# A two-layer hybrid trunk on one core: the triangular inversion starts from 8x8 blocks solved on VectorE, and taps and a rounding go to ScalarE

## The reference

```python
h = rmsnorm(x); proj = h @ w_in          # q,k,v | g_out | a,b | glu | gates
q,k,v = silu(causal_depthwise_conv(qkv, 4 taps)); q,k = l2norm
o = gated_delta_chunked(q, k, v, g, beta)      # 8 heads of width 128
y_a = (rmsnorm(o) * silu(g_out)) @ w_a_out
c = val * sigmoid(gt); c = causal_depthwise_conv(c, 31 taps) + bias
y_b = silu(rmsnorm(c)) @ w_b_out
x = x + (sigmoid(gate_a) * y_a + sigmoid(gate_b) * y_b) @ w_o

# inside gated_delta_chunked, per head and chunk:
m = (k*beta) @ k.T * decay_strict              # strictly lower triangular
sol = triangular_solve(eye + m, [v*beta | k*beta*exp(gc)])
```

## Time and profile before

| | us |
|---|---|
| median of 3 runs | 2707.73 (2707.4 to 2707.75) |
| span of the profiled execution | 2705.9 |
| TensorE busy | 2695.0 |
| VectorE busy | 1583.0 |
| ScalarE busy | 1099.9 |
| GpSimd busy | 257.8 |

### The profile page before, as it was taken

How to read it: one execution, slowest core, us unless ns; L and a number is a source line. 1 busy time by engine, 2 the same in 40 slices (tenths; PEclk the granted TensorE clock), 3 DMA queues, 4 the chain that set the end, 5 groups by cost and what they waited for, 6 DMA issues and landing times.

```text
span 2705.9 us, 35838 instructions
## 1 busy us (share of the span) xinstructions
PE 2695.0 (100%) x13096; PEld 2251.8 (83%) x13096; DVE 1583.0 (59%) x2505; ACT 1099.9 (41%) x1849; POOL 257.8 (10%) x231
## 2 busy tenths in 40 slices
PE   9999999999999999999999999999999999999998
PEld 7888878888888888888888888788888888888887
DVE  6554357888885345554355543688888944455532
ACT  4222246766663232222222222566666633322222
POOL 0000022122120010000000000221211200100000
PEclk9999999999999999999999999999999999999999
DMA  4223335564552223233322233455556432232331
GB/s 167 95 99 104 92 102 141 126 142 115 136 130 93 100 86 101 93 101 94 103 93 93 101 93 95 109 133 137 125 128 141 102 109 96 90 101 93 97 95 66
DMA packets 83482, 292.04 MB, mean 108 GB/s; under 512 B 10032, under 2 KB 10800, under 8 KB 83376
## 3 DMA queue, kind: packets, MB, share of 16 engines
q1 hardware_dynamic: 68112, 235.85, 27.0%
q0 software_dynamic: 14976, 54.53, 11.0%
q10 hardware_dynamic: 288, 0.27, 0.0%
HBM read 233.99 MB, written 2.10 MB: 87 GB/s over the span
## 4 chain that ended last, share of the span: by engine, by line
PE 99%; issue 0%; DVE 0%; DMA 0%; DVEq 0%; SPq 0%; POOLq 0%; ACT 0%; POOL 0%
PE bank L451 97%; PE bank L650 1%; PE bank L702 1%; PE bank L664 0%; PE bank L738 0%; DMA xT<-in_x 0%; PE bank L471 0%; DVE NT L1683 0%; DVE XT L1688 0%; DVE h_lo L1276 0%; DVE y L1351 0%; PE bank L814 0%; DVEq L120 0%; POOLq L120 0%; ACT h_hi L891 0%
## 5 line engine op out<-in xcount | busy, mean ns | idle before, releaser
L1251 DVE TENSOR_TENSOR w_lo<-raw,w_hi 128x1024 fp32r<-128x1024 f32 x342 | 422.8, 1237 | 535.4 <-ACT w_hi L868 535.4
L868 ACT ACTIVATE w_hi<-raw 128x1024 fp32r<-128x1024 f32 x446 | 470.0, 1055 | 651.1 <-PE bank L451 651.0
L451 PE MATMUL bank<-h_hi,w_hi 128*128 128x512 f32 x1504 | 587.5, 391 | 1.1 <-issue 0.6
L451 PE MATMUL bank<-h_hi,w_lo 128*128 128x512 f32 x1504 | 585.6, 389 | 0.0
L451 PE MATMUL bank<-h_lo,w_hi 128*128 128x512 f32 x1504 | 585.3, 389 | 0.0
L451 PE MATMUL bank<-g_hi,w_hi 128*128 128x512 f32 x928 | 382.1, 412 | 0.0
L451 PE MATMUL bank<-g_hi,w_lo 128*128 128x512 f32 x928 | 377.8, 407 | 0.0
L451 PE MATMUL bank<-g_lo,w_hi 128*128 128x512 f32 x928 | 369.4, 398 | 0.0
L451 PEld LDWEIGHTS bank<-h_hi,w_hi 128*128 128x128 f32 x1504 | 282.4, 188 | 63.0 <-issue 2.3
L451 PEld LDWEIGHTS bank<-h_hi,w_lo 128*128 128x128 f32 x1504 | 282.3, 188 | 58.9
L1554 DVE SCALAR_TENSOR_TENSOR cacc<-c_raw,ncol,cacc 128x512 f32<-128x512 f32 x464 | 330.3, 745 | 0.4
(11 more groups left out here) (256 smaller groups left out, 3352.4 us busy)
## 6 DMA issues: line engine op xcount, KB each, us to landing
raw<-in_w_in SPq DMA_DIRECT2D x128, 512.0 KB, 3.3
w_lo<-raw POOLq DMA_DIRECT2D x104, 512.0 KB, 4.6
raw<-in_ffn_w_up SPq DMA_DIRECT2D x88, 512.0 KB, 3.3
raw<-in_ffn_w_gate SPq DMA_DIRECT2D x87, 512.0 KB, 3.3
raw<-in_ffn_w_down SPq DMA_DIRECT2D x64, 512.0 KB, 3.5
raw<-in_ffn_w_down SPq DMA_DIRECT2D x32, 384.0 KB, 3.1
raw<-in_w_a_out SPq DMA_DIRECT2D x16, 512.0 KB, 3.3
raw<-in_w_b_out SPq DMA_DIRECT2D x16, 512.0 KB, 3.3
```

The costliest lines, as they stand in the source:

```text
L451: return nc.tensor.matmul(o, a, b, start=start, stop=stop, **kw)
L868: nc.scalar.activation(w_hi[c % SLOTS][:, :], raw[c % SLOTS][:, :], ACT.Copy).then_inc(hi_done, 1)
L1251: tt(w_lo[c % SLOTS][:, :], raw[c % SLOTS][:, :], w_hi[c % SLOTS][:, :].bitcast(F32), ALU.subtract).then_inc(lo_v, 1)
```

## The change

Levels 0 and 1 go. `BASE` = 2: level 2 finds in bank 0 the inverses of the 8x8 diagonal blocks, made thus: ScalarE copies the 32x32 diagonal blocks of NT (*near*, four copies of 32 partitions each), VectorE masks them to the 8x8 blocks (*diag*), sums them into rows (*cin*) and spreads them over a unit pattern (*own*, 256 elements); one TensorE product with the block mask (*rows*) gives every partition its block's rows in bank 2; back substitution by VectorE (z7, then z6p, z6a to z1p, z1a on 4 to 28 elements) gives X, and X0 writes it to bank 0. Late taps are put between these steps (`inside`, `ahead`), `LATE` becomes 10. The taps 0 and 1 of the long convolution (`first_taps`) and o's rounding (`o_round`) are done by ScalarE, after XT of level 3. attnT and "c" move behind level 2. The constants lose two masks and get one. `transpose`s of `gr` become matmuls with the same operands and one accumulation group.

```diff
-PE_ORDER = "H H gr kt H kk kq H so H H H x2t vt H H H xt0 y0 H H fb xy0".split()
-for _l in range(1, LEVELS):
-    PE_ORDER += ("H H H " if _l < LEVELS - 1 else "H H H H ").split() + f"xt{_l} y{_l} H H H xy{_l}".split()
+PE_ORDER = "H H gr kt H kk kq H so H H H rows vt H H H H H H fb H H H H H H H H".split()
+for _l in range(BASE, LEVELS):
+    PE_ORDER += ("H H H " if BASE < _l < LEVELS - 1 else "H H H H " if _l == LEVELS - 1 else "").split() + f"xt{_l} y{_l} H H H xy{_l}".split()
 PE_ORDER += "H H H xtf H H H vn0 H H os0".split()
 for _c in range(1, NC):
     PE_ORDER += f"H H p{_c} H H vn{_c} H H H os{_c}".split()
 HALVES = 12
-LATE = 8
+LATE = 10
...
-DVE_STEPS = ["hs", "kT", "qT", "dmin", "skE", "rden", "bnk2", "neg", "NT", "x2T", "vT", "yd0", "attnT"]
-DVE_STEPS += [f"yd{_l}" for _l in range(1, LEVELS)]
+DVE_STEPS = ["hs", "kT", "qT", "dmin", "skE", "rden", "bnk2", "neg", "NT", "vT", "diag", "cin", "own"]
+DVE_STEPS += [f"z{SIDE - 1}"] + [f"z{_k}{_x}" for _k in range(SIDE - 2, 0, -1) for _x in "pa"] + ["X0", f"yd{BASE}", "attnT"]
+DVE_STEPS += [f"yd{_l}" for _l in range(BASE + 1, LEVELS)]
 DVE_STEPS += ["vn0", "s0"]
 for _c in range(1, NC):
     DVE_STEPS += [f"r{_c}", f"vn{_c}"] + ([f"s{_c}"] if _c < NC - 1 else [])
-DVE_TAIL = ["og", "vE", "oF", "ohi", "olo"]
-
-ACT_STEPS = ["thk", "thq", "XTI", "thv", "ksq", "eg", "decT", "kd", "n0", "n1"]
-ACT_AFTER = [["n4", "sgc"], ["n2"], ["n3"], ["n5"], ["vs"], []]
-for _l in range(LEVELS):
-    ACT_STEPS += [f"XO{_l}", f"XE{_l}", f"XT{_l}"] + ACT_AFTER[_l]
+DVE_TAIL = ["og", "vE", "oF", "olo"]
+
+ACT_STEPS = ["thk", "thq", "thv", "ksq", "eg", "decT", "kd", "near"]
+ACT_AFTER = {1: ["n3"], 2: ["n5"] * (BASE == 1), 4: ["vs"]}
+ACT_STEPS += ["n2", "n3", "n4", "n5", "sgc"]
+for _l in range(BASE, LEVELS):
+    ACT_STEPS += [f"XO{_l}", f"XE{_l}", f"XT{_l}"] + ACT_AFTER.get(_l, [])
...
+        wide = NC * SIDE
+        near = X[:, 0:NC * QUAD].rearrange("p (c j) -> p c j", c=NC)
+        c_in = X[:, 128:128 + wide]
+        c_out = X[:, 160:160 + wide].rearrange("p (c i) -> p c i", c=NC)
+        part = X[:, 192:192 + wide]
+        own = X[:, 256:256 + SIDE * wide].rearrange("p (r f) -> p r f", r=SIDE)
...
-        NO = [(t, i) for t in (Y, dec, thv) for i in range(2)]
+        NO = {2: (Y, 0), 3: (Y, 1), 4: (thv, 0), 5: (thv, 1)}
+
+        unit_col = cst[:, I_UP, QUAD:QUAD + SIDE]
+        rows = bank[2][:, 0:SIDE * wide].rearrange("p (r c i) -> p c r i", r=SIDE, c=NC)
...
-                    elif name == "x2t":
-                        ve("x2T")
-                        ac("eg")
-                        for c in range(NC):
-                            t = slice(c * P, c * P + P)
-                            m = mm(bank[0][:, t], XT[:, t], ident, start=(c == 0), stop=(c == NC - 1), is_transpose=True)
-                        m.then_inc(*pe_dn.step(name))
+                    elif name == "rows":
+                        ve("own")
+                        mm(bank[2][:, 0:SIDE * wide], cst[:, I_LV, :], own.rearrange("p r f -> p (r f)")).then_inc(*pe_dn.step(name))
...
                 def front(rn):
 
-                    act.wait_ge(pe_dn.sem, pe_dn.after(rn - 1, "vn3"))
-                    nc.scalar.activation(chunked(XT), each_chunk(I_ID), ACT.Copy).then_inc(*ac_dn.step("XTI"))
                     act.wait_ge(ve_ds.sem, ve_ds.after(rn, "v3"))
                     nc.scalar.activation(thv[:, :], va[:, :], ACT.Tanh).then_inc(*ac_dn.step("thv"))
 
-                def head(dense, rn, held):
+                def o_round(rn):
+
+                    act.wait_ge(ve_tl.sem, ve_tl.after(rn, "oF"))
+                    nc.scalar.activation(o_hi[:, rn % HEADS, :], og[:, :], ACT.Copy).then_inc(*ac_tl.step("ohi"))
+
+                def head(dense, rn, held, before=True):
 
                     Rd, c0, rd = dense
                     gates = rd is None
@@ -1090,7 +1100,10 @@
 
                     def halves(lv):
 
-                        pe_(f"xy{lv - 1}" if lv else "x2t")
+                        if lv > BASE:
+                            pe_(f"xy{lv - 1}")
+                        else:
+                            ve("X0")
...
+                    def first_taps():
+
+                        act.wait_ge(ve_cr.sem, ve_cr.after(rn, "craw"))
+                        nc.scalar.activation(cacc[0][:, :], c_raw[:, 0:SEQ], ACT.Identity, bias=ncol[:, PR_B:PR_B + 1], scale=ncol[:, 0:1]).then_inc(taps, 1)
+                        nc.scalar.activation(cacc[1][:, :], c_raw[:, 1:1 + SEQ], ACT.Copy, scale=ncol[:, 1:2]).then_inc(taps, 1)
...
-                    odd_columns(0)
-                    odd_columns(1)
+                    for q in range(P // QUAD):
+                        w = slice(q * QUAD, q * QUAD + QUAD)
+                        a = nc.scalar.activation(near[w], chunked(NT)[w, :, w], ACT.Copy)
+                    a.then_inc(*ac_dn.step("near"))
+                    odd_columns(2)
+                    odd_columns(3)
                     hi(*held)
-                    halves(0)
-                    negative(held[1])
-                    turned(0)
                     ve("vT")
                     odd_columns(4)
+                    odd_columns(5)
+                    negative(held[1])
                     act.wait_ge(ve_tl.sem, ve_tl.after(rn - 1, "og"))
                     act.wait_ge(ve_sg.sem, ve_sg.after(rn, "sg"))
                     nc.scalar.activation(sgc[:, :], sgn[:, :], ACT.Copy).then_inc(*ac_dn.step("sgc"))
-                    halves(1)
-                    turned(1)
                     dense_steps(0, *dense)
-                    ve("attnT")
-                    odd_columns(2)
                     halves(2)
                     turned(2)
-                    odd_columns(3)
                     hi(Rd, c0 + 4, residue=True)
                     halves(3)
                     turned(3)
-                    odd_columns(5)
+                    first_taps()
+                    if before:
+                        o_round(rn - 1)
                     squares(0, 1)
                     dense_steps(1, *dense)
                     hi(Rd, c0 + 5)
...
+                    if k == 1:
+                        o_round(l * 8 + 7)
...
-                    tap, late, summed = [0], [CONV - LATE], [1]
+                    tap, late, summed = [2], [CONV - LATE], [1]
 
                     def long_tap(j, rn, hn):
                         src, acc = c_raw[:, min(j, TAPS - 1):min(j, TAPS - 1) + SEQ], cacc[j % 2]
-                        if j == 0:
-                            dve.wait_ge(ve_cr.sem, ve_cr.after(rn, "craw"))
-                            ts(acc[:, :], src, ncol[:, 0:1], ncol[:, PR_B:PR_B + 1], ALU.mult, ALU.add).then_inc(taps, 1)
-                        elif j == 1:
-                            ts(acc[:, :], src, ncol[:, 1:2], None, ALU.mult).then_inc(taps, 1)
-                        elif j < TAPS:
-                            dve.wait_ge(taps, rn * CONV + (CONV + j - 1))
+                        if j < TAPS:
+                            dve.wait_ge(taps, rn * CONV + (CONV + max(j - 1, 2)))
                             stt(out=acc[:, :], in0=src, scalar=ncol[:, j:j + 1], in1=acc[:, :], op0=ALU.mult, op1=ALU.add).then_inc(taps, 1)
...
-                    behind = [("l", "a", "l", "c"), ("oF", "t", "ohi", "t", "olo", "t"), ((0, 0), "t", (0, 1), "t", (0, 2)),
-                              ("t", "t", "t", "t", "t"), ((1, 0), "t", (1, 1), "t", (1, 2)),
-                              ("t", "t", (2, 0), "t", (2, 1), "t", (2, 2))]
+                    inside = {6: "l", 5: "l", 4: "l"}
+                    ahead = "lll"
+                    behind = {2: ("l", "c", "a", "oF", (0, 0)), 3: ((0, 1), "t", (0, 2), "olo", "t"), 4: ((1, 0), "t", (1, 1), "t", (1, 2)),
+                              5: ("t", "t", (2, 0), "t", (2, 1), "t", (2, 2))}
...
+                    def near_blocks():
+
+                        ac("near")
+                        tt(near, near, cst[:, I_UP:I_UP + 1, 0:QUAD].broadcast_to([P, NC, QUAD]), ALU.mult).then_inc(*ve_dn.step("diag"))
+                        ts(c_out[:, :, SIDE - 1:SIDE], unit_col[:, SIDE - 1:SIDE].rearrange("p (c i) -> p c i", c=1).broadcast_to([P, NC, 1]),
+                           1.0, None, ALU.mult)
+                        me("diag")
+                        nc.vector.tensor_reduce(c_in.rearrange("p (c i) -> p c i", c=NC), near.rearrange("p c (b i) -> p c i b", i=SIDE),
+                                                mybir.AxisListType.X, ALU.add).then_inc(*ve_dn.step("cin"))
+                        me("cin")
+                        tt(own, c_in.rearrange("p (r f) -> p r f", r=1).broadcast_to([P, SIDE, wide]),
+                           unit_col.rearrange("p (r f) -> p r f", f=1).broadcast_to([P, SIDE, wide]), ALU.mult).then_inc(*ve_dn.step("own"))
+
+                    def near_inverse(behind):
+
+                        pe_("rows")
+                        k = SIDE - 1
```

(58 more changed lines are left out.)

3 lines of the change are left out of this document (1 added, 2 removed).

## The result

| us | before | after |
|---|---|---|
| median | 2707.7 | 2736.66 (4 executions, 2733.8 to 2736.8) |
| span of the profiled execution | 2705.9 | 2735.0 |
| mean granted clock | 0.999 | 0.995 |
| TensorE busy | 2695.0 | 2680.4 |
| a middle head, hs to hs | 49.03 | 49.52 |

The change makes the kernel slower by 1.05% (ratio 1.0105, 95% interval 1.0090 to 1.0119). The sign was forecast, the size was not: +29.0 us where +11.9 stood on record, and 2736.7 lies above the range. In these lists of executions the changed kernel scatters by 3 us, the kernel before by 0.4.

A forecast was written before the change was run, and what follows sets the result against it. TensorE's own work was taken as the bound. Per layer -17.0 saved, +8.9 before rows, +6.4 at xt4, +3.4 in rounds 0 and 7, +4.2 at the end: +5.9, +11.9 for two layers, 2719.6 us; range 2698 to 2732.

The forecast's parts named there:

- the clock: TensorE's granted clock, taken as 1.00; closing caveat: if it falls behind the new waits, every number is too small; unsized.
- the leftover tap: VectorE's twentieth tap, run after the last VN, delays the next head by 0.2 us in rounds 2 to 7.
- The wait for rows: TensorE waits 0.73 us before rows for own; with leftover tap and slow start, 8.9 us a layer.
- The wait for xt4: TensorE waits 0.97 us for XO4 behind ScalarE's taps, 1.07 with the start, rounds 1 to 6: 6.4 us a layer.
- TensorE's saving: TensorE's own work from x2t to xt2 shrinks by 2.12 us a head, 33.9 us in 16 heads.
- The chain of z: VectorE's inversion after rows: z7 and twelve steps, 0.22 us apart, ending at 6.0 us; no cost at xt2.
- xy3: TensorE waits there for VectorE's late tap 2: 1.9 us in round 0, 1.25 in round 7.
- The end: End of the convolution in round 7: six taps run after the last VN, column sums wait, 4.2 us a layer.
- The chain to own is short: Rival: overlapping copies, tiny reduction, leftover tap absorbed before rows; half of 17.8 us goes, 2710.7; chance 0.11.
- the ScalarE queue has air: Rival: ScalarE's queued work was waiting for TensorE anyway, so xt4's wait goes; -12.8 us, 2706.8; chance 0.14.
- the slipping chain: Rival: VectorE's 13 steps behind rows run slower, making xt2 late; at 0.40 a step 15 us, 2735; chance 0.08.
- Both queues keep ahead of TensorE: Rival: only the convolution's end and the two odd rounds cost; -18.7 us, 2689; chance 0.17 with all between.

The follow-up runs named there:

- f_dummy4: Changed kernel with four fp32 products of constants put into TensorE's wait before the column sums at each layer's end: 2730.5 us.
- g_all: Changed kernel with first taps before level 3's turn, eleven late taps, near and diag on VectorE, round 7's squares summed on GpSimd: 2705.2 us.
- l_near1: Changed kernel with one 128-partition ScalarE copy for near instead of four, leaving out the right blocks for three quarters of the partitions: 2720.4 us.
- i_three: Changed kernel with three more half products ahead of rows in TensorE's order and three fewer behind fb: 2711.9 us.
- a_swap: Changed kernel with ScalarE's two first taps moved in front of the turn of level 3: 2714.1 us.
- m_swap3: Changed kernel with the two first taps before level 3's turn and three more half products ahead of rows: 2693.3 us, ratio to before 0.9945.
- d_late11: Changed kernel with LATE 11, four of the late taps ahead, so one tap more is carried into the next head: 2729.9 us.
- n_swap3d: Changed kernel with first taps before level 3's turn, three more half products ahead of rows, four constant products in the layer-end wait: 2687.5 us.

## Why the prediction was wrong

**The step that failed most: the clock, a term put at nothing, 11.9 us.** The last sentence of the prediction names the case, but neither the sum, a rival nor the range holds it. The range's upper end was built from cin, near, rows and the leftover tap alone, +11 in all; the clock alone is +11.9, so the range had room for one of the two, not for both. The stops themselves, 1.9 and 4.2, stood in my text. The trace of before has no fall while TensorE works and could not price one; but a bound was due (at the 1.2 GHz level half of the time behind a long stop is lost). f_dummy4, with its forecast of -5.1 and -6.2 measured, shows the cause at the layers' ends (its missing fall in round 0 is in the 6.2). In round 0 no run fills the stop, and the cause rests on the traces: what a fall costs there is measured (1.64), when one comes is not certain. A stop of 4.0 was followed by a fall in 18 of 18 cases (nine kernels, two ends each), one of 1.8 to 1.9 in 15 of 28, eight single ones before rows of 1.3 to 1.6 in none, those of up to 1.2 in none (the program's last microseconds left out). The ends with sums on GpSimd have stops of 1.5, 1.3 and 0.4 close together or a part of them: one fall in eight, in g_all. What else decides between the two outcomes at 1.8 stays open.

**The wait for rows: 0.39 a head too short.** From NT's end (618.28) to rows (620.84) are 2.56 us; my steps made 2.17 (662.99 - 660.82). *near* took 1.27, I had 0.94; *cin* 0.38, I had 0.29. The rest was right to 0.05. I took the overlap of successive ScalarE copies from rows of 256 elements and more, and carried it to 128; l_near1, with one copy in place of four, took 9.9 us off these waits. The Trainium skill (VectorE: DVE Perf Modes, the section on the TRN2 errata) speaks of a fixed latency of each operation from SBUF, exposed between instructions; the trace agrees: copies of 128 elements stand 0.32 apart at 0.31 each, though those of 256 still start 0.10 before the end of the one before. I had cited it and sided with the wrong rows. Against it, the leftover tap came to 0.17 and not 0.2, and the slow start behind rows was 0.05 and not 0.2. The whole stop came to 1.28 in the mean of five middle heads (49.50 less i_three's 48.22; a_swap's 48.46 less m_swap3's 47.18) against 1.13: about 2 us in fourteen heads. Counted from the slot it is 1.36; the difference between heads is less by the 0.06 that xt2 takes in their place.

**The wait for xt4: the steps nearly right, the restart too small.** xt4 started 4.97 behind xt3 (637.52 - 632.55), forecast 4.86: the first scaled tap took 0.10 longer than the 0.71 of the sum. So it was 1.09 late and not 0.97, and the restart took 0.23 and not 0.1. The stop cost 1.32 and not 1.07: 3 us in twelve heads. Of the restart a_swap and m_swap3 still pay 0.2, at a start nearly in time, so moving the taps gives back 1.04 a head and not 1.32 (49.50 - 48.46).

**Right.** TensorE's saving: 49.03 less about 46.9 is 2.1 a head, forecast 2.12. From rows to xt2 7.83, forecast 7.89, but by errors that cancel: rows itself took 0.53 (0.48 where it had not waited) and not 0.3, and vt, fb and the H each a little less than their terms. The chain of z: steps 0.20 apart, done at 627.4 with 1.3 us to spare; i_three spent that spare and gained by it. xy3: 1.82 and 1.18 in brackets, 1.99 and 1.34 from the slot, forecast 1.9 and 1.25. The end: 4.03 in the bracket, 4.2 from the slot (811.01 + 0.22 to 815.43), forecast 4.2. The leftover tap: 0.17 a head from d_late11, forecast 0.2.

Sum: 11.9 forecast, 11.9 for the clock, 2 and 3 for the two stops, -0.5 for round 7, where xt4 does not wait, and 0.5 ahead of the first head (hs at 411.93 instead of 411.46, for which the sum has no term): 28.8 of 29.1 in the spans.

**The rivals.** "The chain to own is short" failed by near, "the ScalarE queue has air" by a queue without a gap, and the slipping chain by steps of 0.20. "Both queues keep ahead of TensorE" did not happen as written. Its number, 2689, is close to n_swap3d's 2687.5, but by other terms: the waits for xy3 are 1.0 there and not 6.8, and each middle head keeps 0.3 at xt2 and xt4.

So the idea was sound, and its placing cost more than it saved. It takes 2.1 us a head from TensorE, and its two new chains start where the old ones did: 1.1 to 1.3 us too late for the old slots, with time unused at their other ends: 1.3 us ahead of xt2, and 0.95 of ScalarE's ahead of XT3.

## What to carry to other kernels

When a change shortens the engine that bounds the kernel, move the slots with it: the idle time that a chain has left behind a slot is exactly what its wait ahead of the slot can be paid from, and here two moves of order turned +1.05% into -0.55%. Price a stop from the slot that was due, not from the recorded wait, and add the clock for the longest ones. Small operations in a row, on either engine, are to be counted at their full durations, as the copies of 128 elements show here.
